# A two-layer decoder trunk on one core: the gated activation is rounded two half pieces later, and the head's mean square of x moves from GpSimd to ScalarE and TensorE

## The reference, cut to what matters

```python
def modulate(x, gain, shift, scale):            # rms_norm: x * rsqrt(mean(x*x) + EPS) * gain
    return rms_norm(x, gain) * (1 + scale) + shift
m = silu(c) @ mod_w + mod_b                      # shift, scale, gate vectors: 14 of 2048 in all

def chunked_sgu(h, ...):                         # layer 0's mixer
    u, v = split(gelu(h @ w_in)); ...; return (u * sv) @ w_out
def conv_ffn(h, ...):                            # both layers
    z = causal depthwise conv of (h @ w_up)
    a, v = split(z);  return (silu(a) * v) @ w_down
```

## Time and profile before

| what | value |
|---|---|
| median of 3 runs | 2706.32 us (2698.91 to 2709.19) |
| span of the profiled execution, first to last instruction | 2699.8 us; no other time is given for it |
| PE busy | 2556.0 us, 95% |
| DVE busy | 2120.2 us, 79% |
| ACT busy | 1237.2 us, 46% |
| POOL busy | 454.1 us, 17% |
| chain that ended last | PE 74%, DVE 12%, DMA 6%, issue 3%, ACT 3%, POOL 2% |
| ACT's stage 3 (L945) | x30, 22 of them idle before for POOL's L1249, 135.4 us together |
| mean granted clock of TensorE | 0.973 |

### The profile page before, as it was taken

How to read it: one execution, slowest core, us unless ns; L and a number is a source line. 1 busy time by engine, 2 the same in 40 slices (tenths; PEclk the granted TensorE clock), 3 DMA queues, 4 the chain that set the end, 5 groups by cost and what they waited for, 6 DMA issues and landing times.

```text
span 2699.8 us, 38453 instructions
## 1 busy us (share of the span) xinstructions
PE 2556.0 (95%) x13984; PEld 2192.4 (81%) x13984; DVE 2120.2 (79%) x2557; ACT 1237.2 (46%) x1638; POOL 454.1 (17%) x229
## 2 busy tenths in 40 slices
PE   3789999998999999999998999999899999999998
PEld 2568888887888888888887889788788888888887
DVE  6967898899888878887789896687987756665665
ACT  2254443444544345534544444483454535453543
POOL 4000110233112011200132400172212101110110
PEclk9899999999999999999999998898999999999999
DMA  7979688886777876787665877406677654555443
GB/s 291 386 305 351 243 324 326 324 325 233 280 267 280 331 263 260 268 316 287 257 237 225 323 279 295 182 2 234 246 280 270 239 193 176 190 193 184 178 178 133
DMA packets 94310, 685.47 MB, mean 254 GB/s; under 512 B 10465, under 2 KB 10465, under 8 KB 11233
## 3 DMA queue, kind: packets, MB, share of 16 engines
q1 hardware_dynamic: 93746, 681.27, 66.7%
q10 hardware_dynamic: 432, 2.38, 0.2%
HBM read 681.51 MB, written 2.10 MB: 253 GB/s over the span
## 4 chain that ended last, share of the span: by engine, by line
PE 74%; DVE 12%; DMA 6%; issue 3%; ACT 3%; POOL 2%; ACTq 0%; DVEq 0%; SPq 0%; POOLq 0%
PE banks L1393 42%; PE banks L1395 21%; DMA raw<-in_stream 6%; DVE w_lo L1034 4%; DVE raw L1050 3%; PE banks L1362 2%; PE banks L1364 2%; PE banks L1365 2%; ACT w_hi L883 1%; PE banks L755 1%; DVE zpad L1130 1%; DVE temp L1098 1%; DVE temp L1140 1%; PE banks L719 1%; PE banks L741 1%
## 5 line engine op out<-in xcount | busy, mean ns | idle before, releaser
L1393 PE MATMUL banks<-h_op,w_hi 128*128 128x512 f32 x3840 | 1373.4, 402 | 42.6 <-DVE w_lo L1034 23.2
L1034 DVE TENSOR_TENSOR w_lo<-raw,w_hi 128x1024 fp32r<-128x1024 f32 x841 | 1072.8, 1300 | 425.4 <-ACT w_hi L883 421.6
L883 ACT ACTIVATE w_hi<-raw 128x1024 fp32r<-128x1024 f32 x841 | 870.5, 1054 | 982.1 <-PE banks L1395 580.8
L1395 PE MATMUL banks<-h_op,w_lo 128*128 128x256 f32 x3840 | 1085.7, 283 | 0.0
L1393 PEld LDWEIGHTS banks<-h_op,w_hi 128*128 128x128 f32 x3840 | 730.8, 190 | 227.1 <-DVE w_lo L1034 27.1
L1393 PE MATMUL banks<-act_op,w_hi 128*128 128x512 f32 x2176 | 772.6, 399 | 11.6 <-POOL act_op L1258 6.8
L1395 PEld LDWEIGHTS banks<-h_op,w_lo 128*128 128x128 f32 x3840 | 735.2, 191 | 0.1
L1395 PE MATMUL banks<-act_op,w_lo 128*128 128x256 f32 x2176 | 613.0, 282 | 0.0
L1050 DVE CUSTOM_DVE_ANT_0 raw<-raw,c_all 128x2048 f32<-128x2048 f32 x224 | 559.1, 2517 | 13.1 <-ACT c_all L869 9.6
L1393 PEld LDWEIGHTS banks<-act_op,w_hi 128*128 128x128 f32 x2176 | 411.4, 189 | 113.9 <-issue 8.4
L1395 PEld LDWEIGHTS banks<-act_op,w_lo 128*128 128x128 f32 x2176 | 414.0, 190 | 0.0
(11 more groups left out here) (149 smaller groups left out, 1392.8 us busy)
## 6 DMA issues: line engine op xcount, KB each, us to landing
raw<-in_stream SPq DMA_DIRECT2D x645, 1024.0 KB, 5.5
x_res<-in_x SPq DMA_DIRECT2D x1, 2048.0 KB, 11.2
out_x<-x_res SPq DMA_DIRECT2D x4, 512.0 KB, 5.1
mix_area<-in_w_s ACTq DMA_DIRECT2D x1, 1024.0 KB, 4.9
mix_area<-in_b_s ACTq DMA_DIRECT2D x1, 1024.0 KB, 8.2
small<-in_small SPq DMA_DIRECT2D x1, 682.0 KB, 16.2
attn_area<-in_pos ACTq DMA_DIRECT2D x1, 273.0 KB, 5.5
c_all<-in_c SPq DMA_DIRECT2D x1, 8.0 KB
```

Of the source, the lines that this page charges most:

```text
L883: act.activation(w_hi[:, out, 0:n], raw[:, slot, half:half + n], ACT.Copy).then_inc(hi_ready, 1)
L1034: dve.tensor_tensor(w_lo[:, out, 0:n], raw[:, slot, half:half + n], w_hi[:, out, 0:n].bitcast(F32), ALU.subtract).then_inc(stream, 2 if ch ...
L1393: pe.matmul(banks[:, g + j, :], hi[:, k, P * j:P * (j + 1)], operand[:, kt, :], start=(kt == 0), stop=False, skip_group_check=True)
L1395: last = pe.matmul(banks[:, g + j, 0:T], lo[:, k, P * j:P * (j + 1)], operand[:, kt, 0:T], start=False, stop=(kt == last_kt), skip_group_c ...
```

## The change

- `PAT`: in P0, P2 and P3 the fourth E (stage 3) stands behind s6 and s7 instead of ahead of them. The order of the splits and modulation pieces among themselves stays, and so does that of the stream. On DVE stage 3 is empty, save for `mix_weights` in the first chunk of `sgu_u0`.
- The head's mean square: after silu(c) ACT squares x in four instructions of 128 x 1024 into the two halves of `temp`, the third and fourth when PE has read the first and second; PE sums each with four matmuls of 256 columns against ones, 16 in all, in its order behind the spreading of c; ACT takes the root at once. DVE's reciprocal comes behind the sixth modulation piece. POOL does nothing for the head; its sums for the later three h stay.

```diff
--- before.py
+++ after.py
@@ -79,9 +79,9 @@
 
 
 PAT = {
-    "P0": "sssEsEsEsEss",
-    "P2": "sssEsEsEsmEssm",
-    "P3": "sssEsEsEsmmEssm",
+    "P0": "sssEsEsEsssE",
+    "P2": "sssEsEsEsmssEm",
+    "P3": "sssEsEsEsmmssEm",
     "F2": "sssEsEsEsEssmm",
     "F3": "sssEsEsEsEssmmm",
     "Q0": "sssEEsEsEs",
@@ -349,6 +349,8 @@
         mod_moved = sem("mod_moved")
         mod_ready = sem("mod_ready")
 
+        x_squared = sem("x_squared")
+        x_squares_read = sem("x_squares_read")
         xsq = sem("xsq")
         xhalf = sem("xhalf")
         xquarter = sem("xquarter")
@@ -869,6 +871,18 @@
             act.activation(c_all[:, :].rearrange("p (b n) -> p b n", b=4), banks[:, 4:8, :], ACT.Silu) \
                 .then_inc(c_ready, 1)
 
+            act.wait_ge(x_loaded, 16)
+            for q in range(QUARTERS):
+
+                if q >= 2:
+                    act.wait_ge(x_squares_read, q - 1)
+                act.activation(temp[:, q % 2, :], x[:, TPC * q:TPC * (q + 1), :].rearrange("p k t -> p (k t)"),
+                               ACT.Square).then_inc(x_squared, 1)
+            act.wait_ge(summed, 1)
+            act.wait_ge(consts_set, 1)
+            act.activation(rstd[:, :], banks[:, 0, 0:T], ACT.Sqrt, scale=1.0 / D, bias=eps[:, :]) \
+                .then_inc(rms_ok, 1)
+
             def split_hi(cur, u, tok):
 
                 off, chunk = cur.first.piece_of[tok], cur.first
@@ -885,15 +899,11 @@
             def make_h(name, tiles, fresh, ready):
 
                 i = h_index(name)
-                if fresh:
+                if fresh and name != "head":
                     k = STAT_ORDER.index(name)
-                    if k == 0:
-                        act.wait_ge(x_loaded, 16)
-                    act.wait_ge(xhalf, 3 * (k + 1))
+                    act.wait_ge(xhalf, 3 * k)
                     for j in range(TPC):
-                        if k:
-
-                            act.wait_ge(xlow, TPC * BY_NAME[X_FROM[name]][3].n["xup"] + j + 1)
+                        act.wait_ge(xlow, TPC * BY_NAME[X_FROM[name]][3].n["xup"] + j + 1)
                         act.activation(y4[:, j, :], x[:, 3 * TPC + j, :], ACT.Square).then_inc(squared, 1)
                     act.wait_ge(summed, k + 1)
                     act.wait_ge(consts_set, 1)
@@ -1077,14 +1087,19 @@
                     dve.scalar_tensor_tensor(out=out, in0=out, scalar=1.0, in1=small[:, g:g + n], op0=ALU.add,
                                              op1=ALU.mult).then_inc(mod_ready, 1)
 
+            def invert_rms(k):
+
+                dve.wait_ge(rms_ok, k + 1)
+                dve.reciprocal(rstd[:, :], rstd[:, :]).then_inc(rstd_ok, 1)
+
             def make_h(name, tiles, fresh, ready):
 
                 i = h_index(name)
                 shift, scale, _ = H_OF[name]
                 if fresh:
                     k = STAT_ORDER.index(name)
-                    dve.wait_ge(rms_ok, k + 1)
-                    dve.reciprocal(rstd[:, :], rstd[:, :]).then_inc(rstd_ok, 1)
+                    if k:
+                        invert_rms(k)
                     dve.wait_ge(rstd_ok, k + 1)
                 dve.wait_ge(mod_ready, ready)
                 if name == "q":
@@ -1174,6 +1189,8 @@
                     elif t == "m":
                         mod_piece(cur, m, tok)
                         m += 1
+                        if name == "head" and first and m == 6:
+                            invert_rms(0)
                     else:
                         if first and e == 0:
                             for k in FINISHED.get(name, []):
@@ -1210,12 +1227,9 @@
 
                 if q == 3:
                     return
-                n = 3 * k + q
-                if k == 0:
-                    pool.wait_ge(x_loaded, 16)
-                else:
-                    name = STAT_ORDER[k]
-                    pool.wait_ge(xlow, TPC * (BY_NAME[X_FROM[name]][q].n["xup"] + 1))
+                n = 3 * (k - 1) + q
+                name = STAT_ORDER[k]
+                pool.wait_ge(xlow, TPC * (BY_NAME[X_FROM[name]][q].n["xup"] + 1))
                 tiles = x[:, TPC * q:TPC * (q + 1), :].rearrange("p k t -> p (k t)")
                 if n:
                     pool.wait_ge(xhalf, n)
@@ -1231,9 +1245,6 @@
                     pool.tensor_copy(gt[:, 0:256], gt[:, 256:512]).then_inc(xsum, 1)
                 else:
                     pool.tensor_tensor(gt[:, 0:256], gt[:, 0:256], gt[:, 256:512], ALU.add).then_inc(xsum, 1)
-
-            for q in range(3):
-                sum_squares(0, q)
 
             pool.wait_ge(mix_loaded, 32)
             pool.affine_select(out=w_sT, in_=w_sT, compare_op=ALU.is_ge, fill=0.0, base=0,
@@ -1315,6 +1326,12 @@
                 spread = pe.matmul(banks[:, 4 + b, :], ones[0:1, :], c_all[0:1, 512 * b:512 * (b + 1)], start=True,
                                    stop=True)
             spread.then_inc(c_spread, 1)
+            for q in range(QUARTERS):
+                pe.wait_ge(x_squared, q + 1)
+                for j in range(TPC):
+                    last = pe.matmul(banks[:, 0, 0:T], ones[:, :], temp[:, q % 2, T * j:T * (j + 1)],
+                                     start=(q == 0 and j == 0), stop=(q == QUARTERS - 1 and j == TPC - 1))
+                last.then_inc(summed if q == QUARTERS - 1 else x_squares_read, 1)
 
             def step(name, cur, prev, first):
                 kind = cur.first.kind
@@ -1324,14 +1341,13 @@
                 free_wait(pe, cur)
                 if name == "sgu_u0" and cur.first.loc == 1:
                     mix_pe(g)
-                if first and name in H_OF and H_OF[name][2]:
+                if first and name in H_OF and H_OF[name][2] and name != "head":
 
                     k = STAT_ORDER.index(name)
-                    pe.wait_ge(consts_set, 1)
-                    pe.wait_ge(xsum, 3 * (k + 1))
+                    pe.wait_ge(xsum, 3 * k)
                     pe.matmul(banks[:, 0, 0:T], ones[:, :], gt[:, 0:T], start=True, stop=False)
                     for j in range(TPC):
-                        pe.wait_ge(squared, TPC * k + j + 1)
+                        pe.wait_ge(squared, TPC * (k - 1) + j + 1)
                         last = pe.matmul(banks[:, 0, 0:T], ones[:, :], y[:, T * j:T * (j + 1)], start=False,
                                          stop=(j == TPC - 1))
                     last.then_inc(summed, 1)
```

## The result

| | before | after |
|---|---|---|
| median of the runs on one chip | 2704.52 us (2698.91 to 2709.19, 4 runs) | 2655.32 us (2651.77 to 2656.08, 4 runs) |
| span of the profiled execution | 2699.8 us | 2654.3 us |
| mean granted clock | 0.973 | 0.975 |

After / before is 0.9824, 95% interval [0.9802, 0.9846]: 49 us by the medians, 45.5 by the spans. Three later comparisons give 0.982, 0.9831 and 0.9841. The forecast was 2666, 40 us less than before.

What follows compares the result with a forecast made beforehand. PE, busy 95% of the span, was taken to bound the kernel, so only its waits or late start could be won. Head 13 plus rounding 27 gave 40 us: 2706.3 - 40 = 2666, range 2650 to 2692.

Steps and rivals of the forecast that it cites:

- Head, 13 us: Mean square moved from POOL to ACT and PE: first norm at 35.6 instead of 48.74, 13.1 us won.
- if the sums are done before the sixth piece: Head's favourable bound: reciprocal runs from 26.7 to 28.5, norm stands at 33.6, a gain of 15.1 us.
- Rounding, 27 us: Splits of s6 and s7 ahead of the gated product's rounding: 29 us from stalls less 2.4 of costs.
- the term of 1.64 a stall: Up phases: each of eleven PE stalls at s6 costs 1.64 us, 18 us together, clock falls counted separately.
- as they read: Pricing the eleven stalls at their traced waits of 1.85 to 2.19 us; with clock falls 33 us, not 29.
- The cost of 2.4: First chunks of `sgu_o0` and `sgu_o1`: PE waits for POOL's low half, 1.2 us in each phase.
- The turn behind the first modulation piece: Up step: POOL's product gets SBUF after DVE's first modulation piece, ahead of the second, from 715.0 to 717.2.
- the first rival: DVE keeps the way to SBUF, POOL's product ends at 721.9, s0 stalls 1.3 us: 2686; chance 0.16.
- The margin of that next s0: Up step: next chunk's s0 low half is ready at 725.4, PE needs it at 726.0, 0.6 us to spare.
- the fourth rival: Slower: work behind the rounding stalls the next chunk's s0, 5.4 us each if POOL is shut out: 2741; chance 0.05.
- the second: Rival: s6's half piece lands late at 717.82, so no earlier split is possible; 2695, chance 0.07.
- the third: Rival: the head's gain is lost through slower PE records or the stream's hole being cover; 2679, chance 0.08.

## Why the prediction was right, and where its sizes were off

The mechanism of both parts was as put; the gain was 43 to 49 us in four comparisons where 40 stood.

**Head, 13 us.** The norm came at 34.10, not 35.6. The step that was mis-sized is PE's sums: I took 0.42 us a record, 13.3 in all, from the earlier trace rows, where eight matmul records run on an engine that had idled; 32 of them in a row took 8.88, 0.28 each (8.57 to 10.16 in the other traces with the new head). The first eight did cost 0.43 each (3.48 us busy from 14.5 to 18.0, x8), as in the earlier trace rows; the others cost about 0.22 (5.40 from 18.0 to 23.5, x25). The granted clock reads 1.00 in both windows, so it does not show what halved them, and that stays open. The root was over at 23.9 instead of 28.6, and the reciprocal waited for nothing: it began at 27.33 behind the sixth piece. That is the bound "if the sums are done before the sixth piece", with 33.6 for the norm and 34.10 measured. Of the 14.6 us at the norm 12.2 were left at the end of the head: the hole in the stream closed to 2.2 us, not to one, and the stream is what the head ends on. Alone this part measured 14.4. The 3.0 us that the sgu phases add in the profiled pair are not its doing: from the first matmul of `sgu_u0` to PE's sum of squares before layer 0's first up phase the stretch took 344.4 us before and 341.6 after, 341.2 with the head alone changed, and 337.5 with P2 alone, which leaves the head and the patterns of this stretch as before.

**Rounding, 27 us.** Forecast were 29 from eleven stalls and -2.4 in `sgu_o0` and `sgu_o1`; alone it measured 30.9. As they read the stalls sum to 21.8, the seven falls of the clock to 11.0, the stall in `dn00` is 0.3 shorter, and one fall of 1.57 behind it is new: 31.5. The four stretches of the table that hold the stalls give 7.6 + 9.9 + 9.3 + 5.9 = 32.7. So the term of 1.64 a stall was too small and "as they read" was nearer. I had set the 46.83 us between two stalls against a period of 45.19 from another part of the trace, and the hi matmuls there do not last the same (391 ns in the mean between these stalls, from 723 to 765, and 398 in the stretch of the earlier trace rows). By the spacing of the matmuls' starts a chunk takes 22.19 us from 723 to 862 and 22.61 from 2004 to 2092. Each against its own, the stalls cost 46.83 - 2 x 22.19 = 2.45 where one read 2.18, and 47.34 - 2 x 22.61 = 2.12 where one read 1.86: 0.26 more than they read. The 1.57 for the fall of the clock stands, since both stretches that it is taken from ran at 22.19. The faster matmuls do not come with the stalls, which stand in stretches of either kind. They also spread the gain over the table: up to `dn00` the kernel before ran six chunks in 22.19 where the kernel after took 22.61, 2.5 us that hide a part of its gain there. The cost of 2.4 did not appear.

**`dn00` and `dn01`: the stall stays.** 1.93 and 1.92 us, where about 2.2 was forecast. That the modulation pieces hold it was right, but not the whole: with one moved POOL's own low half still leaves 1.00, and with all moved it is gone from s6 and comes back at s0.

**The turn behind the first modulation piece.** It was the step on which the first rival hung, and held: 6.56 us, and PE never waited at s6 or at the next s0. The margin of that next s0 (0.6 us by my sum) was not used up anywhere. Without the modulation piece the product took 4.35, with the same time of the kernel. The first and the fourth rival did not happen; the second and the third are excluded by the two halves measured apart.

**What I had called signs.** The norm near 36 (34), no hole (2.2 us), POOL idle until the mask, no wait at s6 in the up phases, `w_lo` waits near 6 (7.4), all came. The clock rose only from 0.973 to 0.975, no more than executions of the kernel after differ by among themselves (0.973 to 0.977): it is at 0.50 from 30 to 41 us, where it was 1.00, and the compressed blocks had more of the half clock (below). In the eleven traces with the new head it falls between 26 and 30 us, while PE idles between its sums and the first split (23.4 to 38.97 in the kernel after). Idling alone does not explain it: in the kernel before PE idled from 9.8 to 41.9 at a granted clock of 1.00. Why it falls here and not there is open.

## What to carry to other kernels

When an in-order engine stands still for a result, look at what is queued behind it that could go first, and at where the result's own consumer really needs it: here two splits cost nothing ahead of the rounding and removed 20 us of PE's waits. But the same place filled with two modulation pieces more in every P3 chunk shifts the wait to the next chunk's first operand, and costs 32 us; count the pieces that then stand in a row. Take a stall's price as it reads, with a little on top (0.26 us here), plus the fall of the clock behind it, and compare two stretches only when their matmuls last the same. Take the price of a run of small matmuls from a run, not from the first few behind a pause.

## What the runs showed of the hardware

- At the same granted clock of 1.00 the same matmul has two durations. From 315 to 360 us, by form (count, busy us, mean ns), in the kernel after:

```profile
L1409 PE MATMUL banks<-h_op,w_hi 128*128 128x512 f32 x125 | 44.2, 399 | 0.0
```

and with the reciprocal late, the same stretch:

```profile
L1409 PE MATMUL banks<-h_op,w_hi 128*128 128x512 f32 x122 | 42.3, 394 | 0.0
```

A chunk there takes 22.61 us or 22.19, 1.9% apart, and the traces with the short one (head alone, P2 alone, reciprocal late) share no edit. It changes inside an execution, from stretch to stretch: 0.42 us a chunk, so a dozen chunks make 5 us that are no kernel's (an estimate from these two periods). What sets it is open.
- Where PE does the compressed blocks' narrow matmuls (behind 1578 us in the kernel after) the granted clock is at half for 20.5 to 30.7 us in the fourteen traces, with PE busy throughout: 20.5 in the trace before, 27.3 after. Work that takes 6.8 us more at half the clock costs 3.4 us, which fits the -3.7 us of the table. The length follows no edit: with POOL busy in the head it is 20.5, and 27.3 to 30.7 in the other traces of the kernel after. The window of the kernel after, columns as above:

```profile
1580.00:1612.00 32.00, 32.00 (x154) 30.72 (x154) 12.85 (x13) 14.48 (x15) 0.00 (x0) 0.61 0.58 211
```

- POOL's product of 128 x 1024 took 6.56 to 6.66 us with one or two modulation pieces behind s5 on DVE and 4.35 to 4.45 without one, though `w_lo` subtractions with two inputs were there in both.
